# Two transformer blocks on one core: the seams between products, the end of the differential attention, the index scores and the first softmax of the sparse mixer are written in another order

## What is computed

```python
# first network, layer i (0: conformer convolution, 1: differential attention)
h = h + conformer_conv(u, ...)           # ends in u @ w_pw2 + b_pw2  ("pw2")
h = h + diff_attention(u, ...)           # 8 heads, ends in o @ w_o   ("wo")
u = rms_norm(h, ffn_norm_g[i])
h = h + swiglu(u, w_gate, w_up, w_down)  # "up0a/b", "down0a/b", "up1..", "down1.."
gate = sigmoid(rms_norm(h, ple_norm_g[i]) @ ple_w_gate[i])
h = h + gate * (p[i] @ ple_w_proj[i])    # "ple0", "ple1"
# differential attention, each head h
w = probs[:, :, 0] - lam * probs[:, :, 1];  o = rms_norm(w @ v, sub_g) * (1 - lambda_init)
# second network, layer 0: x is scaled and shifted, then the sparse mixer
h = x * (1.0 + sc_m) + sh_m;  z = h @ w_in      # "e_index", "e_qk", "e_v", "e_conv", "e_gate"
score = sum over 8 index heads of relu(q_idx @ k_idx) * w_idx     # top 128 keys are kept
ya = softmax over the kept keys of q @ k, times v                # attention("dsa")
yb = bg * causal_dwconv(cg * xb, conv_w)                         # the gated half
y = concat([ya, yb]) @ w_out                                     # "e_out"
```

## Time and profile before

| | |
|---|---|
| Runs | 2722.18 us median, 2721.81 to 2744.45 |
| Profiled execution | 2721.14 us, its span 2719.3 us |
| Mean granted clock | 0.973 |
| PE busy | 2550.2 us, 94% |
| DVE, POOL, ACT busy | 1561.1 (57%), 1097.9 (40%), 1046.6 (38%) |

### The profile page before, as it was taken

The page is one execution under the profiler, slowest core; times in us unless marked ns, Lnnn a source line. Parts: engine busy times, 40 slices in busy tenths (PEclk is TensorE's granted clock), DMA queues, the critical chain, the costliest instruction groups (busy, mean ns, idle before and its releaser), DMA issues.

```text
span 2719.3 us, 29928 instructions
## 1 busy us (share of the span) xinstructions
PE 2550.2 (94%) x11024; PEld 1992.8 (73%) x11024; DVE 1561.1 (57%) x1937; ACT 1046.6 (38%) x1375; POOL 1097.9 (40%) x378
## 2 busy tenths in 40 slices
PE   7979999998999699999989989899998999899997
PEld 5747888876777478888776867688886746688886
DVE  5986756755445467477538554662554354662553
ACT  5444322234565442222334233642334333542342
POOL 6834444433343243443432453244433243344442
PEclk9989999999999899999999989999998999999999
DMA  5215546523221155564342311233322111223321
GB/s 154 63 39 147 183 147 195 161 85 110 67 61 66 39 165 176 157 190 141 89 119 78 93 47 55 67 89 101 105 74 90 59 62 39 70 83 104 99 84 63
DMA packets 398588, 273.35 MB, mean 101 GB/s; under 512 B 11107, under 2 KB 380771, under 8 KB 398476
## 3 DMA queue, kind: packets, MB, share of 16 engines
q1 hardware_dynamic: 384652, 221.55, 28.4%
q10 hardware_dynamic: 13824, 50.34, 5.0%
HBM read 269.74 MB, written 2.12 MB: 100 GB/s over the span
## 4 chain that ended last, share of the span: by engine, by line
PE 77%; DVE 8%; issue 7%; ACT 4%; POOL 3%; SPq 0%; DMA 0%; DVEq 0%; ACTq 0%; POOLq 0%
PE ps L653 23%; PE ps L654 22%; PE ps L655 22%; POOL weight_lo L1985 3%; DVE ps L1743 2%; PE ps L844 1%; PE ps L914 1%; PE ps L813 1%; PE ps L1114 1%; PE ps L829 1%; PE ps L1023 1%; ACT weight_hi L2099 1%; PE ps L1069 1%; PE ps L1124 1%; PE ps L809 1%
## 5 line engine op out<-in xcount | busy, mean ns | idle before, releaser
L1985 POOL TENSOR_TENSOR weight_lo<-weight_raw,weight_hi 128x2048 fp32r<-128x2048 f32 (+2 forms) x224 | 923.1, 4121 | 1403.1 <-ACT weight_hi L2099 1403.1
L653 PE MATMUL ps<-u_hi,weight_hi 128*128 128x512 f32 x2336 | 931.4, 399 | 93.2 <-DVE u_lo L1221 43.1
L654 PE MATMUL ps<-u_lo,weight_hi 128*128 128x512 f32 x2336 | 917.3, 393 | 0.0
L655 PE MATMUL ps<-u_hi,weight_lo 128*128 128x512 f32 x2336 | 916.7, 392 | 0.0
L2099 ACT ACTIVATE weight_hi<-weight_raw 128x2048 fp32r<-128x2048 f32 (+2 forms) x224 | 383.2, 1711 | 572.3 <-PE ps L655 537.8
L653 PEld LDWEIGHTS ps<-u_hi,weight_hi 128*128 128x128 f32 x2336 | 443.6, 190 | 208.2 <-DVE u_lo L1221 53.0
L654 PEld LDWEIGHTS ps<-u_lo,weight_hi 128*128 128x128 f32 x2336 | 444.0, 190 | 95.9 <-issue 5.1
L655 PEld LDWEIGHTS ps<-u_hi,weight_lo 128*128 128x128 f32 x2336 | 443.4, 190 | 94.0
L653 PE MATMUL ps<-act_hi,weight_hi 128*128 128x512 f32 x704 | 274.4, 390 | 2.0 <-DVE act_lo L1189 2.0
L655 PE MATMUL ps<-act_hi,weight_lo 128*128 128x512 f32 x704 | 273.9, 389 | 0.0
L654 PE MATMUL ps<-act_lo,weight_hi 128*128 128x512 f32 x704 | 273.9, 389 | 0.0
(11 more groups left out here) (293 smaller groups left out, 2527.4 us busy)
## 6 DMA issues: line engine op xcount, KB each, us to landing
weight_raw<-in_ffn_w_up SPq DMA_DIRECT2D x132, 512.0 KB, 5.3
arena<-in_ada_w ACTq DMA_DIRECT2D x96, 512.0 KB, 5.8
weight_raw<-in_ffn_w_down SPq DMA_DIRECT2D x64, 704.0 KB, 4.6
weight_raw<-in_ffn_w_gate SPq DMA_DIRECT2D x44, 512.0 KB, 4.0
weight_raw<-in_ev_w_in SPq DMA_DIRECT2D x10, 1024.0 KB, 5.3
weight_raw<-in_conv_w_pw SPq DMA_DIRECT2D x16, 512.0 KB, 5.5
weight_raw<-in_ple_w_gate SPq DMA_DIRECT2D x16, 512.0 KB, 3.7
weight_raw<-in_attn_w_qkv SPq DMA_DIRECT2D x16, 512.0 KB, 5.1
```

The costliest lines, as they stand in the source:

```text
L653: pe.matmul(bank, w[0], x[0], start=start, stop=False)
L654: pe.matmul(bank, w[0], x[1], start=False, stop=False)
L655: return pe.matmul(bank, w[1], x[0], start=False, stop=stop)
L1985: pool.tensor_tensor(w_lo[r][:, 0:width], raw[r][:, 0:width], w_hi[(k0 + j) % HI_RING][:, 0:width].bitcast(F32), ALU.subtract).then_inc(w_ ...
```

## The change

It has six parts. (1) `stage_gemm(drain=True)` for pw2, ple0 and ple1: the last step runs chunk by chunk over both banks and counts `x_free` after each chunk, so ACT and DVE write the next operand's chunks 0 to 5 while the last step runs. In ple, step 0's four short products of the second bank (`p_hi`) move ahead of the wait for the last operand chunk. (2) The sums of squares are kept in PSUM bank 5, without a memset; behind down0b and down1b each operand chunk is made as soon as its residual chunk is; scaled adds are done in place in PSUM. (3) The operand of e_index is built in ACT and two PSUM banks. (4) At the end of the differential attention the last heads' transposes and statistics use banks 4 to 6, chunks 0 to 4 of wo go at i = G, chunk 5 and the first three of wo's second step at i = G+1, and DVE makes low halves between the pieces of the last `mix`; POOL holds wo's weights back until `mixed`; ACT takes the last two roots together. (5) The index ReLU is in place in PSUM, DVE reads it there, and PE waits for DVE. (6) `mixer_gains` moves ahead of e_gate, and the gated half's operands move into the softmax's iterations 0 (ACT) and 1, 2 (DVE).

```diff
+        def turned_bank(g, kc):
+            return (4 if g == HEADS - 1 else 2) + kc % 2
+        def stat_bank(g):
+            return 6 if g >= HEADS - 2 else 2
...
+                def drained():
+                    w = slot_of(name, Step(last))
+                    banks = [open_tile(t0, Step(last), 2, i) for i in range(2)]
+                    for k in range(DC):
+                        for i in range(2):
+                            if kc[i] == DC:
+                                mm = product(banks[i], cols(w, i, k), x[i](k), k == 0, k == DC - 1)
+                                if k == DC - 1:
+                                    mm.then_inc(tile_done, 1)
+                        if k < DC - 1:
+                            mm.then_inc(x_free, 1)
+                    if kc[1] < DC:
+                        for k in range(kc[1]):
+                            mm = product(banks[1], cols(w, 1, k), x[1](k), k == 0, k == kc[1] - 1)
+                        mm.then_inc(tile_done, 1)
                 def body(st):
...
+                    if k == order[-1] and kc[1] < DC:
+                        for q in range(kc[1]):
+                            product(banks[1], cols(w, 1, q), x[1](q), q == 0, q == kc[1] - 1)
...
+                rest(name, body, last - 1 if drain else last)
+                if drain:
+                    drained()
...
-                    if i == G + 1:
-                        for k in range(G - 2):
-                            out_chunk(k)
-                    if i == G + 2:
-                        out_chunk(G - 2)
...
+                    if i == G:
+                        for k in range(G - 3):
+                            out_chunk(k)
+                    if i == G + 1:
+                        out_chunk(G - 3)
+                        for k in range(3):
+                            out_chunk(k, 1)
+                for k in range(3, G - 2):
+                    out_chunk(k, 1)
+                for j in range(2):
+                    for k in (G - 2, G - 1):
+                        out_chunk(k, j)
                 pe.wait_ge(ln_done, l0 + G)
...
+                stage_gemm(f"ple{i}", (xu, lambda k: (chunk(p_hi, k), chunk(p_lo, k))), kc=(DC, 2), stat=rms_stat, drain=True)
...
-                        pe.wait_ge(relu_done, n.next(relu_done))
+                        pe.wait_ge(relu_used, item - 3)
...
+                dve.wait_ge(squared, q0 + c + 1)
+                dve.wait_ge(summed, s0 + 1 + c)
+                if c == 0:
+                    dve.tensor_copy(square_sum_bank, sq[0]).then_inc(summed, 1)
+                else:
+                    dve.tensor_tensor(sum2 if c == DC - 1 else square_sum_bank, square_sum_bank, sq[c % 2], ALU.add).then_inc(summed, 1)
...
-                        link(dve.tensor_tensor(t, bank, rinv[0], ALU.mult))
-                        dve.tensor_tensor(hc, t, hc, ALU.add).then_inc(tile_used, 1)
+                        link(dve.tensor_tensor(bank, bank, rinv[0], ALU.mult))
+                        dve.tensor_tensor(hc, bank, hc, ALU.add).then_inc(tile_used, 1)
...
+                    early = DC - 2 if name == "pw2" else 0 if name == "wo" else DC
+                    for c in range(DC):
+                        if c == DC - 2 and early == DC - 2:
+                            for k in range(early):
+                                operand_low(k)
+                        body(Step(c))
+                        if early == DC:
+                            if c >= DC - 2:
+                                sums_add(c, base)
+                            operand_low(c)
+                    if early == 0:
+                        sums_add(DC - 2, base)
...
+                        return
+                    if c % 2:
+                        dve.tensor_copy(chunk(u_hi, c), full_bank[1]).then_inc(half_chain, 1)
+                        dve.wait_ge(half_chain, (c + 1) // 2)
+                    dve.tensor_tensor(chunk(u_lo, c), full_bank[c % 2], chunk(u_hi, c).bitcast(F32), ALU.subtract).then_inc(x_ready, 1)
+                for j in range(DC - 1):
+                    scale(j)
+                    if sums and j:
+                        sums_add(j - 1, base)
+                    add(j)
+                if sums:
+                    sums_add(DC - 2, base)
+                for c in range(DC - 2):
+                    operand_low(c)
+                scale(DC - 1)
+                operand_low(DC - 2)
+                add(DC - 1)
+                if sums:
+                    sums_add(DC - 1, base)
+                operand_low(DC - 1)
...
+                        if g == G - 1:
+                            for k in ((0, 1), (2,), (3,), (4,))[b]:
+                                low_u(k, i0 + k + 1, chunk(act, k))
...
-                    if i == G + 1:
-                        for g in range(G - 2):
-                            low_u(g, i0 + g + 1, chunk(act, g))
...
-            i0, _ = n.take(hi_done, DC), n.take(x_ready, DC)
-            for c in range(DC):
-                low_u(c, i0 + c + 1)
...
-                        link(dve.tensor_scalar(sc, act_tmp[i % 2][:, 0:nk], w_col, None, ALU.mult))
...
+            mixer_gains()
...
-            for t in range(4):
-                low_u(4 + t, i0 + t + 1, chunk(act, E_CV + t))
-            mixer_gains()
-            attention("dsa")
+            def gated_low(g, first=i0):
+                if g in (1, 2):
+                    for t in (2 * g - 2, 2 * g - 1):
+                        low_u(4 + t, first + t + 1, chunk(act, E_CV + t))
+            attention("dsa", gated_low)
...
+                            if i == HEADS:
+                                pool.wait_ge(mixed, 4 * HEADS)
...
                     for c in range(DC):
+                        if name == "wo" and c == DC - 1:
+                            sc.wait_ge(tile_done, t0 + DC)
+                            for k in range(DC - 1):
+                                operand_high(k)
+                        if name == "pw2" and c == DC - 2:
+                            for k in range(DC - 2):
+                                left_chunk(k)
+                                operand_high(k)
+                        wait(Step(c))
...
+                        if name.startswith("down") or (name == "wo" and c == DC - 1):
+                            operand_high(c)
...
-                    if i == G + 1:
-                        for g in range(G - 2):
-                            finished(g)
...
+                    if i == G:
+                        sc.wait_ge(tile_done, stages["v3"][2] + 2)
+                        for g in range(G - 3):
+                            finished(g)
...
-                    if 0 <= i - 3 < G:
-                        root = chunk(act, 8 + i - 3)
+                    for g in {G + 1: (), G + 2: (G - 2, G - 1)}.get(i, (i - 3,) if i >= 3 else ()):
+                        root = chunk(act, 8 + g)
...
+                    def operand_half(c):
+                        src, scale, shift = chunk(h, c), mod[:, 8 + c:9 + c], mod[:, c:c + 1]
+                        if c < DC - 1:
+                            left_chunk(c)
+                        if c % 2 == 0:
+                            link(sc.activation(chunk(u_hi, c), src, ACT.Identity, bias=shift, scale=scale))
+                        if c >= 2:
+                            sc.wait_ge(x_ready, x0 + c - 1)
+                        sc.activation(full_bank[c % 2], src, ACT.Identity, bias=shift, scale=scale).then_inc(hi_done, 1)
+                    link.begin(0)
+                    sc.wait_ge(mod_ready, 1)
+                    for c in range(DC - 2):
+                        operand_half(c)
+                    gate(Step(DC - 1))
+                    operand_half(DC - 2)
+                    sc.wait_ge(tile_used, BANKS + t0 + 2 * DC)
+                    operand_half(DC - 1)
+                    split_after("ple1", Step(DC - 1))
                     break
...
-                for c in range(DC):
+                def operand_high(c):
+                    sc.activation(chunk(u_hi, c), chunk(h, c), ACT.Copy, scale=pcol("attn_norm_g", c)).then_inc(hi_done, 1)
+                n.take(x_ready, DC)
...
-                        split_after("ple0", Step(c))
+                    split_after("ple0", Step(c))
                     if c >= 1:
                         square(c - 1)
-                n.take(x_ready, DC)
-                sc.wait_ge(tile_done, t0 + 2 * DC)
-                for c in range(DC):
-                    if c == 3:
-                        square(DC - 1)
-                    if c == DC - 1:
-                        sc.wait_ge(tile_used, BANKS + t0 + 2 * DC)
-                    sc.activation(chunk(u_hi, c), chunk(h, c), ACT.Copy, scale=pcol("attn_norm_g", c)).then_inc(hi_done, 1)
+                square(DC - 2)
+                for c in range(DC - 2):
+                    left_chunk(c)
+                    operand_high(c)
+                gate(Step(DC - 1))
```

(16 more changed lines are left out.)

155 lines of the change are left out of this document (70 added, 85 removed).

## The result

The changed kernel takes 2682.81 us (median of four runs, 2680.43 to 2705.64) against 2721.99 us for the kernel before (four runs): 0.9863 of it, 95% interval 0.982 to 0.9907. Forecast were 2685. The profiled execution has a span of 2680.4 us, 38.9 less than before. (Some executions of either kernel, such as those of 2744.45 and 2705.64 us, are some 23 us longer.)

The account below looks back on a forecast made before the run. PE was taken as the bound (77% of the chain of work), with all gains in its waits; nine terms summed to 36.4 us off the profiled 2721.14, forecast 2685 us, own range 2676 to 2694 (55%), wider range 2672 to 2702.

Parts of the forecast that it names:

- Short seams (pw2, ple0, ple1): Seams pw2 to up0a, down0b to ple0, down1b to ple1: idle gaps close, gaining 1.6, 3.3 and 4.8 us.
- nothing is costed for the PSUM sums: Sums of squares: DVE work beside PE, not locked with a PSUM input, so no term; uncovered, 0.7 us a chunk.
- Step 0 begins some 0.8 us after ple0's end: qkv seam: chunks 0 to 5 are ready, so PE starts almost at once; the seam's term was 4.5 us.
- End of the attention: Differential attention's end to wo's end: 17.2 us earlier, less 5 for clock, so 12.2, between 8 and 17.2.
- (b): Attention's tail: the head's last DVE step is locked under a moved POOL split, the transposes' copy waits; PE idles 4.9 us.
- (e): Inside wo: step 2's weights are rounded only when step 0 has finished, 8.9 us in all; PE idles 4.8 us.
- (c): Attention's tail: wo's chunk 5 and three chunks of step 1, eight pieces or 5.4 us, fill most of a 6.78 us idle.
- First softmax: First softmax: L1631 follows the logits at once, POOL's pass is bound by its own split; 7.6 us, between 6 and 8.4.
- The tail gives almost nothing: Rival: new waits at the attention's end cut its term to 5.8 or 1.2 us; 2692 to 2702, chance 21%.
- only the gaps close: Rival: weights, sums or root set the pace after each seam, so only idles close; 2703.6 us, chance 9%.
- The locks move along: Rival: moved DVE operations start under POOL splits at all nine places, 41.4 us against 36.4; 2726; slower or no gain 4%.
- No clock is lost: Rival: counts without any clock loss give 45.5 us, so 2675.6; chance of below 2676, 11%.

Follow-up runs that it names:

- sums_in_sbuf: Changed kernel with the running sum of squares kept in SBUF instead of PSUM bank 5; its trace ends 4.1 us later in all.
- qk0_two_banks: Changed kernel, but qkv's first product waits for all of ple0's tiles except the last two; 5.2 us gained at the second step, 4.1 where the attention's tail begins.
- tail_stat_earlier: Changed kernel with one chunk of wo's second step, not three, ahead of the last statistic; 2.8 us gained at wo's end, span 4.8 us longer.
- e_index_split_first: Changed kernel, but ACT rounds e_index's second weight slot ahead of the last ple1 gate and last two operand chunks; 5.2 us gained there.
- relu_in_sbuf: Changed kernel with the index ReLU written to SBUF again and PE waiting for ACT; span 2687.9 us, 7.4 longer.
- only_tail: Kernel before with only the changed kernel's end of the differential attention (banks and engine order); that part gained 14.7 us.
- only_mixer: Kernel before with only the changed kernel's index scores and first softmax; span 2710.3 us.
- four_edits: Changed kernel with qk0_two_banks, e_index_split_first, tail_copy_first and tail_stat_earlier together; 2663.31 us, 0.9782 of the kernel before.
- tail_copy_first: Changed kernel with head 5's last step and its low and high halves behind the copies of head 7's transposes; 6.6 us gained by wo's end.

## Why the prediction was right, and where not

The total is better than its parts. The 4.5 us of the qkv seam did not come, and 1.6 us at ple0 and 3.7 us outside the change made up for them, which is luck. The other terms came within 0.8 us of the forecast, by the waits that it names.

- **Short seams (pw2, ple0, ple1).** Right by the trace: the 1.60 and both 2.22 us went, the ple stages' second step no longer waits. No run takes these edits by themselves, so their 11.9 us rest on where the traces part. Too small at ple0: bank waits inside its steps went too, and "nothing is costed for the PSUM sums" was the step that failed. I read them as DVE work beside PE, though the earlier trace rows show what 4.67 us of such an operation do to whatever is queued behind it. `sums_in_sbuf` prices them at 1.5 us inside ple0 and 4.7 at the seam behind it.
- **ple0 to qkv.** "Step 0 begins some 0.8 us after ple0's end" is the step that failed. I had taken that from the operands' times and not from every wait that stands ahead of the first product. 4.5 us were forecast, none came: the six low halves that moved ahead of the last chunk made that wait as long as the idle they were to close. `qk0_two_banks` shows that without it the operands give 5.2 us at the second step and 4.1 where the tail begins, with 1.60 of idle at the last sum for the 2.0 forecast.
- **End of the attention.** 12.4 for 12.2, and by its own steps: (b) an idle of 4.45 for 4.9, through the lock and the copy queued behind; (e) 4.50 for 4.8, through the third weight slot. The last operand chunk came 2.4 us later than counted, and from there to wo's end it took 2.4 longer: 4.8 together, where 5 were taken for the clock. The two slow stretches, with PE busy for 6.41 and 4.53 us, lost half of that, 3.2 ahead of that chunk and 2.3 behind. (c), the eight pieces, held back the last statistic as well, as `tail_stat_earlier` shows.
- **wo to up1a.** -0.4 for -1.2: the idle is 2.04 for 2.3, and none of the 0.5 for clock was lost in this execution.
- **e_index.** Idle 3.34 for 3.7, and the slow stretch behind it cost 1.9 for 1.8 (the 5.2 of `e_index_split_first` less 3.34): right. The weights were there 0.6 us sooner than counted (1380.49, with the 24.55 us gained until then 1405.0 for 1405.6), hence 2.1 for 1.5.
- **Index scores.** 1.6 for 2.1. e_qk begins 16.4 us after the first DVE pass (1407.44 to 1423.86), where 15.95 were counted: between the rows of passes stands a masking step that the count left out (L1884, twice 0.29 us), and a pass of 512 columns, 0.75 us long, follows the one before it only after 0.90 us. Whether a pass costs more with its input in PSUM depends on its form. Seven of eight don't, the plain multiplications do, first before and then after:

```profile
L1819 DVE SCALAR_TENSOR_TENSOR act<-tmp,small,act 128x512 f32<-128x512 f32 x7 | 5.3, 752 | 1.0
...
L1817 DVE TENSOR_SCALAR act<-tmp,small 128x512 f32<-128x512 f32 x1 | 0.5, 487 | 0.0
```

```profile
L1881 DVE SCALAR_TENSOR_TENSOR act<-ps,small,act 128x512 f32<-128x512 f32 x7 | 5.3, 750 | 1.0
...
L1879 DVE TENSOR_SCALAR act<-ps,small 128x512 f32<-128x512 f32 x1 | 0.8, 751 | 0.0
```

  The Trainium skill's rule on PSUM operands ("VectorE: DVE Perf Modes", "Why PSUM operands drop a tier") agrees with the plain multiplication, 487 ns from SBUF and 751 from PSUM. The prediction's 0.25 us for such a pass was right (0.26), and it had been covered by its 0.751 us a pass. (Three times 0.25 would have made 2685.5, not 2685.2.)
- **First softmax.** Right to 0.2 us; POOL's pass begins at the end of its split, as counted:

```profile
1558.05 4.54 POOL L2051 TENSOR_TENSOR weight_lo<-weight_raw,weight_hi 128x2048 fp32r<-128x2048 f32 x1 [6.27 <-ACT weight_hi L2167]
1562.57 0.60 POOL L2064 TENSOR_SCALAR arena<-arena,small 128x128 f32<-128x128 f32 x1
```

- **The rivals.** "The tail gives almost nothing" and "only the gaps close" fell by the table. "The locks move along" was true at one place, the step of 3.22 us. "No clock is lost" was wrong inside, but behind the changed parts, where the programs are equal, the kernel before has slow stretches that the changed one lacks: 2.8 us, which no edit made. (Its 45.5 us also counted 0.8 for the softmax's low halves as clock; without them they are 44.7.)

## What to carry to other kernels

An operand that is ready early is worth what the last of all waits ahead of its first use allows: list every wait at that place, the ones that the diff leaves alone too, and what the diff has put ahead of the work they wait for. Ask of each step that moves what it starts beside; here a DVE operation with two SBUF inputs was 0.7 us or up to 5, by whether POOL was splitting weights, and one PSUM input for the sums was worth 6.2 us at ple0 and the seam behind it. When a wait is closed, look for the next thing in the same program order (here the rounding of the next weights) before counting the gain.

## What the hardware showed that I had not expected

The same program can lose its clock or not. In the latent attention of the second block's second layer, where both kernels do the same work after the same idles, the kernel before has 6.8 us at half clock and the changed one has none in its like stretch (columns as in the earlier trace rows):

```profile
2218.70:2225.50 6.80, 6.80 (x20) 3.74 (x21) 2.52 (x6) 2.10 (x7) 3.23 (x3) 0.50 0.01 2
```

```profile
2180.00:2186.80 6.80, 5.99 (x33) 3.71 (x33) 3.21 (x8) 4.24 (x13) 4.30 (x5) 1.00 0.00 0
```

The code that stands there doesn't decide it. `relu_in_sbuf`, which has the changed kernel's code there, loses its clock from 2187.3 to 2194.1 and with it 2.9 us; `only_tail` and `only_mixer`, which have the code of the kernel before, don't. In the same way the idle of 2.04 us at wo's end costs nothing more in the changed kernel, and 1.6 us of slow clock in `e_index_split_first`, `tail_stat_earlier` and `four_edits`. I had read from the earlier trace rows that short gaps cost no clock; they can.

A second stretch varies more, between 254 and 390 us. There DVE weighs rows of `ada_w` as they land (18 operations with two SBUF inputs). In the kernel before they take 1.28 us; in `only_tail`, whose own edit lies 500 us further on, 3.26 us, with 25 us of waiting ahead of them, nearly all for the DMA:

```profile
L1349 DVE SCALAR_TENSOR_TENSOR arena<-arena,small 128x1024 f32<-128x1024 f32 x18 | 23.0, 1279 | 2.2 <-DMA arena<-in_ada_w 1.0 <-DVE arena L1349 0.9
```

```profile
L1365 DVE SCALAR_TENSOR_TENSOR arena<-arena,small 128x1024 f32<-128x1024 f32 x18 | 58.7, 3261 | 25.0 <-DMA arena<-in_ada_w 23.8 <-DVE arena L1365 0.9
```

PE is 24.3 us later behind this stretch than ahead of it, against the trace before, and 23.6 in `tail_copy_first` against the changed kernel. A likely chain is that a DMA which lands late pushes these operations under POOL's splits, and what is queued behind them on DVE reaches PE late. No run tested it.
